# Mixture-of-experts decoder on eight cores: overflow rows gathered five blocks ahead, and one shared tile for the last slots of four experts

## The reference, cut to what matters

```
def hierarchical_moe(xn, ...):
    g_idx = argmax(t @ rg_w + rg_b)                       # one of 4 groups
    top_v, top_i = top_k(e_logits of that group, 2)       # 2 of its 8 experts
    top_w = softmax(top_v) * softmax(g_logits)[g_idx]
    for e in range(32):
        hdn = silu(t @ w_gate[e]) * (t @ w_up[e])         # 1024 -> 256
        out += (hdn * combine[:, e:e+1]) @ w_down[e]      # 256 -> 1024
```

## Time and profile before

| | |
|---|---|
| median of 3 runs | 2522.89 us (2522.39 to 2526.45) |
| the profiled execution's own time | 2530.44 us |
| its span on core 4, the slowest (others from 2506.3) | 2529.2 us |
| PE busy / weight loads / DVE / ACT / POOL | 65% / 45% / 38% / 32% / 17% |
| mean granted TensorE clock, core 4 | 0.794 |
| q0 (POOL's DMAs), q1 (SP's), share of 16 engines | 37.8%, 8.5% |

### The profile page before, as it was taken

One profiled execution on the slowest core, in us unless ns is written; L12 is line 12 of the kernel. 1 busy time (PEld: TensorE's weight loads), 2 busy tenths in 40 slices (PEclk: granted clock), 3 DMA queues, 4 the chain that ended last, 5 costly groups with the idle time before them and its releaser, 6 DMA issues.

```text
span 2529.2 us, 39086 instructions; the slowest of 8 cores (2506.3 to 2529.2 us)
## 1 busy us (share of the span) xinstructions
PE 1654.4 (65%) x12979; PEld 1143.6 (45%) x12979; DVE 960.4 (38%) x2379; ACT 811.8 (32%) x1615; POOL 432.7 (17%) x476
## 2 busy tenths in 40 slices
PE   1899964343688788641877888884433688788643
PEld 1678752112455455431764445442211455565432
DVE  0556553444122122261653444343443322222255
ACT  1444422321233233322324443442232233233333
POOL 2000001113222222334000000000111322222220
PEclk9899986566888888855988888887655789989855
DMA  8900043014799699579000000006101699999464
GB/s 165 281 2 1 1 66 80 34 50 101 161 206 195 143 194 195 149 231 152 11 1 1 1 1 1 1 1 111 42 34 50 127 211 184 197 193 188 140 223 140
DMA packets 98939, 269.48 MB, mean 107 GB/s; under 512 B 34438, under 2 KB 47110, under 8 KB 90296
## 3 DMA queue, kind: packets, MB, share of 16 engines
q0 software_dynamic: 61712, 193.45, 37.8%
q1 hardware_dynamic: 37032, 73.55, 8.5%
HBM read 521.67 MB, written 111.67 MB: 250 GB/s over the span
## 4 chain that ended last, share of the span: by engine, by line
PE 49%; DMA 18%; DVE 17%; issue 8%; ACT 5%; DVEq 1%; POOL 1%; another core or an unknown queue 0%; ACTq 0%; SPq 0%; POOLq 0%
DMA sb_xo<-xs,sb_o_rx 12%; PE psb L755 8%; PE psb L365 7%; PE psb L910 7%; PE psb L774 4%; PE psb L502 4%; PE psb L734 3%; DVE sb_xnC L291 2%; DVE sb_xn L291 2%; PE psb L840 2%; PE psb L417 2%; PE psb L1091 2%; PE psb L278 2%; DVE sb_z L833 2%; DMA sb_w_in<-w_in 2%
## 5 line engine op out<-in xcount | busy, mean ns | idle before, releaser
L365 PE MATMUL psb<-sb_xnA,sb_w_in 128*128 128x256 bf16 (+1 forms) x1728 | 188.8, 272 | 43.3 <-DMA sb_w_in<-w_in 39.7
L133 POOL DMA_DIRECT2D sb_we<-wcat x64 | 36.6, 574 | 993.5 <-ACT sb_sq L272 880.4
L743 ACT ACTIVATE sb_xT<-psb 128x640 bf16<-128x640 bf16 (+1 forms) x128 | 83.2, 650 | 358.0 <-PE psb L734 244.9
L365 PEld LDWEIGHTS psb<-sb_xnA,sb_w_in 128*128 128x128 bf16 x1728 | 165.4, 100 | 63.1 <-issue 43.6
L745 DVE COPY sb_xT<-psb 128x640 bf16<-128x640 bf16 (+1 forms) x128 | 58.6, 458 | 318.2 <-PE psb L774 255.3
L762 DVE TENSOR_TENSOR sb_hd<-psb,sb_sil 128x320 bf16<-128x320 f32 (+1 forms) x128 | 58.7, 458 | 309.5 <-PE psb L755 178.6
L755 PEld LDWEIGHTS psb<-sb_xT,sb_wov 128*128 128x128 bf16 x2048 | 148.1, 113 | 57.4 <-issue 57.3
L502 PE MATMUL psb<-sb_xn,sb_wr 128*36 128x256 f32 (+1 forms) x272 | 100.0, 551 | 109.1 <-DVE sb_xn L291 96.4
L755 PE MATMUL psb<-sb_xT,sb_wov 128*128 128x128 bf16 x2048 | 154.7, 245 | 24.3 <-DVE sb_xT L745 14.1
L272 ACT ACTIVATE sb_sq<-sb_h 128x256 bf16<-128x256 f32 (+2 forms) x408 | 130.7, 396 | 118.9 <-PE psb L278 92.9
L755 PE MATMUL psb<-sb_xT,sb_we 128*128 128x160 bf16 x2048 | 155.6, 235 | 2.5 <-DVE sb_xT L745 1.6
(11 more groups left out here) (169 smaller groups left out, 3090.9 us busy)
## 6 DMA issues: line engine op xcount, KB each, us to landing
sb_we<-wcat POOLq DMA_DIRECT2D x64, 1536.0 KB
ys<-sb_ym SPq DMA_DIRECT2D x64, 512.0 KB
sb_xg<-xs SPq DMA_DIRECT2D x64, 256.0 KB, 5.8
xs<-sb_zrow POOLq DMA_DIRECT2D x1, 10240.0 KB, 97.7
ys<-sb_yh SPq DMA_DIRECT2D x64, 128.0 KB
outT<-sb_ob SPq DMA_DIRECT2D x8, 1024.0 KB, 4.5
sb_h<-xT POOLq DMA_DIRECT2D x7, 1024.0 KB, 49.9
sb_w_in<-w_in POOLq DMA_DIRECT2D x8, 768.0 KB, 24.3
```

The lines of the kernel that those rows point to most:

```text
L365: tr.op("pe", lambda e: e.matmul(ph(bank, half, n), lhsT=w_in[:, c, part * D + j * 128: part * D + (j + 1) * 128], rhs=xn[p2][:, c, :n], s ...
L743: tr.op("act", lambda e: e.activation(out=o_, in_=in_, func=AF.Copy), reads=[], writes=[xTB[s], PB[hf]])
```

## The change

It does six things.

- `xo` has five buffers instead of two, and its gather for block j + 5 is issued in `XT` of block j, ahead of that round's `DN`. The weights `wov` of a block keep two buffers; their gather for j + 2 now goes out ahead of the scatter of block j.
- The slots are numbered anew: 32 x 128 rows first, then 32 x 32. The last 32 slots of four experts are then 128 rows in a row; they are loaded as one tile `xh`, transposed once with eight transposes, and four copies hand each expert its 32 columns. `xT` has five buffers, and blocks have three of their own, `xU`. A block's or expert's 128 columns are copied in one instruction.
- For the new numbers `PLACE` has two more DVE instructions per tile.
- `we` has three buffers instead of four: three experts' weights are loaded before routing, 29 in the loop.
- `overflow_setup` and POOL's clearing of `xo` and `wov` stand before the barrier: the first right behind the last tile's routing, the second before the first tile's.
- The outputs of `yh` and of blocks share three buffers, and the down product takes its four matmuls in another order.

```diff
@@ PLACE
+                V(lambda e: e.scalar_tensor_tensor(out=T("tt"), in0=T("pos"), scalar=128.0, in1=row(c_rest, 32),
+                                                   op0=ALU.is_ge, op1=ALU.mult))
+                V(lambda e: e.tensor_tensor(out=T("val"), in0=T("val"), in1=T("tt"), op=ALU.add))
@@ phase_moe
-                NW = 4
+                NW, NXO, NXT = 3, 5, 5
...
+                for i in range(NXO):
+                    tr.op("pool", lambda e: e.memset(xo[i][:], 0.0), writes=[xoB[i]])
+                for i in range(2):
+                    tr.op("pool", lambda e: e.memset(wo[i][:], 0.0), writes=[woB[i]])
...
+                    O = overflow_setup(s2, l, o_rx, o_rw)
                     tr.barrier()
...
-                    load_x(0)
-                    load_x(1)
-                    for i in range(2):
-                        tr.op("pool", lambda e: e.memset(xo[i][:], 0.0), writes=[xoB[i]])
-                        tr.op("pool", lambda e: e.memset(wo[i][:], 0.0), writes=[woB[i]])
-                    O = overflow_setup(s2, l)
...
+                    def load_x(e):
+                        p = e % 3
+                        if e % 4 == 0:
+                            g, q = e // 4, (e // 4) % 2
+                            tr.dma("sp", "xh%d" % q, [(xh[q][:].bitcast(U16), xs[4096 + g * 128:4096 + (g + 1) * 128, :], xsB, [xhB[q]])])
+                        tr.dma("sp", "xg%d" % p, [(xg[p][:].bitcast(U16), xs[e * 128:(e + 1) * 128, :], xsB, [xgB[p]])])
...
+                    for j in range(NXO):
+                        load_xo(j)
+                    for j in range(2):
+                        load_wo(j)
...
+                    def turn(src, sB):
+                        b = nxt[0] % 2
+                        nxt[0] += 1
+                        pv = ps[:, b * 512:b * 512 + 512].bitcast(BF16)
+                        for c in range(NCH):
+                            tr.op("pe", lambda e: e.transpose(out=pv[:, c * 128:(c + 1) * 128], in_=src[:, c * 128:(c + 1) * 128],
+                                                              identity=identb[:]),
+                                  reads=[sB, cB], writes=[PB[b]])
+                        return b, pv.rearrange("p (c x) -> p c x", c=NCH)
...
                     def XT(k):
                         kind, i = seq[k]
+                        if kind == "o":
+                            b, pv = turn(xo[i % NXO], xoB[i % NXO])
+                            take("dve", xU[i % 3][:], pv, xUB[i % 3], b)
+                            if i + NXO < J:
+                                load_xo(i + NXO)
+                            return
+                        if i % 4 == 0:
+                            g = i // 4
+                            b, pv = turn(xh[g % 2], xhB[g % 2])
+                            for r in range(4):
+                                s = (i + r) % NXT
+                                take("act" if r % 2 else "dve", xT[s][:, :, 128:CAP], pv[:, :, 32 * r:32 * r + 32], xTB[s], b)
+                        b, pv = turn(xg[i % 3], xgB[i % 3])
+                        take("act", xT[i % NXT][:, :, 0:128], pv, xTB[i % NXT], b)
+                        if i + 3 < NE:
+                            load_x(i + 3)
...
@@ DN(k)
-                            for half in range(2):
-                                for f in range(2):
+                            for f in range(2):
+                                for half in range(2):
...
+                            if i + NW < NE:
+                                load_w(i + NW)
                         else:
...
+                            if i + 2 < J:
+                                load_wo(i + 2)
+                            tr.idma("yo%d" % q, [(ys[:], O["rx"][:, i:i + 1], yh[q][:].bitcast(I32), True, NSLOT - 1,
+                                                  [yhB[q], O["B"]], [ysB[2 + p]])])
```

More of the change, by code:

```diff
@@ L655, in phase_moe @@
                 woB = [Buf("wov%d" % i) for i in range(2)]
+                xo = [sb(st_, "xo%d" % i, [128, D], BF16) for i in range(NXO)]
+                xoB = [Buf("xo%d" % i) for i in range(NXO)]
+                o_rx = sb(st_, "o_rx", [128, J], I32)
+                o_rw = sb(st_, "o_rw", [128, J], I32)
                 def load_w(e):
@@ L682, in phase_moe @@
                     ym = [sb(s2, "ym%d" % i, [128, D], F32) for i in range(2)]
[L683 to L684 removed]
                     ymB = [Buf("ym%d" % i) for i in range(2)]
[L686 to L687 removed]
+                    yh = [sb(s2, "yh%d" % i, [128, D], F32) for i in range(3)]
@@ L689, in load_x @@
+                    yhB = [Buf("yh%d" % i) for i in range(3)]
+                    nyh = [0]
+                    nxt = [0]
                     def load_x(e):
-                        p = e % 2
-                        tr.dma("sp", "xg%d" % p, [(xg[p][:].bitcast(U16), xs[e * CAP:e * CAP + 128, :], xsB, [xgB[p]]),
-                                                  (xh[p][:].bitcast(U16), xs[e * CAP + 128:(e + 1) * CAP, :], xsB, [xgB[p]])])
-                    load_x(0)
-                    load_x(1)
@@ L704, in load_o @@
                         tr.idma("wo%d" % p, [(wo[p][:], O["rw"][:, j:j + 1], wcat_d[l][:], False, NE * 128 - 1, [O["B"]], [woB[p]])])
-                    load_o(0)
-                    load_o(1)
+                    for e in range(3):
+                        load_x(e)
+                    for j in range(NXO):
+                        load_xo(j)
+                    for j in range(2):
+                        load_wo(j)
                     seq = []
-                    J = NOV[l]
                     done = 0
@@ L724, in XT, with take @@
+                    def take(eng, out, in_, oB, b):
+                        if eng == "act":
+                            tr.op("act", lambda e: e.activation(out=out, in_=in_, func=AF.Copy), reads=[], writes=[oB, PB[b]])
+                        else:
+                            tr.op("dve", lambda e: e.tensor_copy(out=out, in_=in_), reads=[], writes=[oB, PB[b]])
                     def XT(k):
                         kind, i = seq[k]
-                        i, n, w_, wB_, xB_ = of(k)
-                        s = k % 2
```

97 lines of the change are left out of this document (37 added, 60 removed).

## The result

The changed kernel is slower. Its median is 2549.98 us (4 runs, 2544.83 to 2553.71), that of the kernel before in the same session 2524.59 us; the ratio is 1.010, 95% interval 1.0074 to 1.0125. Forecast were 2494 us, in a range of 2462 to 2527. The profiled execution took 2553.64 us (span 2552.1 us, core 7).

What follows compares the result with a forecast made beforehand. DMA was taken to bound the expert loop, PE second. Routing +11, set-up -2, loops +3 and -6, tails -20 and -15 summed to -29 us: 2494 us from a median of 2522.89, 8-in-10 range 2462 to 2527.

Steps and rivals of the forecast that it cites:

- So the engines should not run dry, and their share rises: Expert loops: while PE waits for `wov`, the next weights are already queued, so DMA share rises to 0.97.
- rival 3: Both expert loops: DMA share stays at 0.94 and 0.89; sum +5 us, 2528 us; chance 13%.
- rival 2: Gate-up waiting for `wov` each period: low clock makes PE the bound, up to +101 us, 2633 us; chance 7%.
- The `xo` wait goes, `wov` is late next: PE in the expert loops: nearly all 148 us of `xo` waits go; blocks then wait for `wov`, some 3 us each.
- DMA bounds the loop, PE is second: Expert loop: an expert costs 12.7 us of all 16 engines, a PE period without a wait 10.1 us.
- rival 4: Both expert loops: engines entirely full, share 1.0; sum -52 us, 2471 us; chance 15%.
- Rival 1: Expert loops: PE sets the pace, period 9.3 instead of 13.2 us, -218 us, about 2313 us; chance 5%.
- Prefetch depth alone gives nothing: Expert loop: with DMA the bound, asking earlier gives nothing that the engines have not in hand.
- Routing, +11: Routing: two more DVE instructions of 0.33 us in each of 17 tiles, +11 us with nothing hiding it.
- worth nothing in the loop, only at its end: Four-in-one tile: PE's period falls from 10.1 to 9.3 us, all under the 12.7 us of DMA.
- Tails, 17 us: End of each loop after the last weights: 17 us instead of 37 and 32, so -20 and -15 us.
- Set-up, -1 per layer: Set-up before the barrier: starts 7.6 us earlier, first x loads cost 7.3; -2 us in all, ends 0 and -4.

Runs made afterwards that it cites:

- e1: The changed kernel with separate tracking entries for the stores of `yh`, so they no longer wait for `ym`'s stores; 2506.0 us, 0.9889 of the kernel before.
- f1: The changed kernel, store wait kept, with two tiles for `yh` and two for blocks' outputs instead of three shared; 2503.97 us, 0.9883 of the kernel before.
- f7: The kernel before with only the gathers of `xo` issued five blocks ahead; 2533.6 us, 1.0029 of the kernel before.
- e3: e1 with the gathers of `xo` two blocks ahead instead of five; 2513.85 us, 0.9941 of the kernel before.
- e1_again: e1 word for word, run on the third chip; 2512.8 us, 0.995 of the kernel before.
- g3: e1 with sixteen transposes per expert, in two halves with a copy each, and `xh` loaded per expert; 2532.8 us, 1.000 of the kernel before.

## Why the prediction was wrong

**The step that failed** is "So the engines should not run dry, and their share rises". It rests on a walk along PE and POOL ("with POOL some 6 us") that leaves out ACT and SP, and the sum has no term for what they do. The change has six listed parts, and five of them have a price; the sixth, that `yh` and the blocks' outputs share three buffers, has none, not even nothing with the work that hides it, and the split of the store was not noticed at all. SP's queue was read for its bytes, 21.2% of the engines, and never walked for its order. Walked, it has a second store with an entry that the first one writes, and the one question left would have been how long a store takes to land there. What the runs showed in its place: a store that waits 13.4 us for the one before it, a tile that comes back after 25.0 us, POOL held 8.05 us before the scatter, and a share of 0.88. The cost of the missing term is what e1 takes away, 2.1% by its first run and 1.5% by the repeat, 38 to 53 us. The range could not hold it, since its upper end came from rival 3, in which the engines do not get fuller; here they got emptier. "Wrong it would be if the share fell though waits remain" did come true, 0.88 instead of 0.97. So did the sign of rival 2, a clock clearly below 0.87: 0.84 in the windows of the slowest core. But PE was busy only 98.69 of 145 us there, e1 without the wait is back at 0.92 and 0.88, and f1 was fast on a core at 0.84; the low clock came with the waits and is not shown to cost anything of its own.

**What was right**, as the versions without that wait show:

- *The `xo` wait goes, `wov` is late next.* In the changed kernel `wov` has only 45 us. In e1 it is 191 us in 51 waits, 3.7 us each; "some 3 us each in most periods" was forecast.
- *DMA bounds the loop, PE is second.* e1's share is 1.00 or 1.01 on its slowest core, above the 0.97 of the forecast and equal to rival 4, "entirely full". Rival 1 (PE sets the pace) and, without the wait, rival 2 (low clock) did not come: e1's clock in the two windows is 0.92 and 0.88, before it was 0.87 and 0.89 in the loops.
- *"Prefetch depth alone gives nothing".* f7: 1.0029. But the depth was not needed to end the wait for `xo` either, as e3 shows.
- *Routing, +11.* Over seven intervals 4.6 us were forecast per layer. By the medians of the eight cores the last seven take 189.6 us in layer 0, before 185.9, and 191.9 in layer 1, before 186.6: 3.7 and 5.3 us.

**What was right by luck.** The sum forecast -29 us. e1's ratio makes -28 us of the 2524.59 us on the first chip and, as `e1_again`, -13 us on the third, with intervals from -37 to -4. The -28 is no proof of the terms: the shared tile brought some 13 us that the sum has at nothing, and the tails brought 10 us less than it has.

**Terms that were off:**

- *The shared tile: "worth nothing in the loop, only at its end".* g3 against `e1_again`: some 13 us in the whole with intervals that still overlap, so likely not nothing. In the two traces 2 us per layer of it lie before the first gate-up (47.2 and 46.2 us against 45.1 and 44.3 from the last tile's routing product); in the loops it is 10.4 us in layer 0 and 1.9 in layer 1, no more than such columns can differ by chance.
- *Tails, 17 us.* With the stores' wait they were 31 and 23 us at 0.32 and 0.21. In e1 about 24 us in layer 0 (1021 to 1045 us) and 20 in layer 1, against 32 and 37 before: the gain is some 25 us of the forecast 35.
- *Set-up, -1 per layer.* From the start of the last tile's routing product to the first gate-up it was 47.1 us in both layers and is 44.9 and 44.3 (medians of the eight cores): -2.2 and -2.8 us, together -5.0, a little outside the ends of 0 and -4 that were given for both.

## What to carry to other kernels

When one request is split into two, or two pools of tiles are made one, ask what the code that sets the waits now puts in order, and compare the way round a tile (wait, transfer, copy) with the time until the ring comes back to it; a wait that costs nothing beside one ring can cost 2% beside a smaller one. Walk every queue that the diff touches in order, the store queue too, even where its share of the bytes is small. Try the new order of a list at the old depth before adding buffers: with the gather ahead of the scatter, depth two had no wait for `xo`. And where neither PE nor the DMA engines are full, look for a dependency before a resource: the chain of waits named it here in its first entry.

## What the runs showed of the hardware

Three things I had not expected. A store of 512 KB on SP's queue took 13.4 us to land, beside weight loads on POOL's queue (the 16 engines were 0.99 busy in those us), and the store of 128 KB behind it another 7.7 us (0.97 busy); so a fourth of the bytes still took more than half of the time. The 16 engines of a core can be held at a share of 1.00 over 340 us by these loads (e1, slowest core: 201 GB/s), where I had taken 0.97 as all that there is. Shares of 1.01 also occur, so the figure is good to one per cent at best. And the spread of the yardstick itself: with the kernel before on the same chip, the same kernel gave 0.9889 on one and 0.995 on another, more than several of the effects looked for, with intervals that just overlap, so that chips and executions are not told apart.
